# First four merge levels of a triangular inverse on 32x32 blocks at four places of TensorE's array, and three small edits around it

## What is computed

```python
def gated_deltanet(h, w_in, conv_w, a_log, dt_bias, norm_w, w_out):
    proj = h @ w_in                                   # q, k, v, z and two small gates
    ...
    q = l2norm(q) * (GDN_HEAD_DIM ** -0.5)
    k = l2norm(k)
    ...
    o = chunk_gated_delta_rule(q, k, v, g, beta)
    o = o * lax.rsqrt(jnp.mean(o * o, axis=-1, keepdims=True) + RMS_EPS) * norm_w
    o = o * jax.nn.silu(z)
    return o @ w_out

def chunk_gated_delta_rule(q, k, v, g, beta):
    ...
    m = jnp.where(strict, jnp.einsum("bhnid,bhnjd->bhnij", k_beta, k) * decay, 0.0)
    a_mat = jnp.eye(CHUNK, dtype=q.dtype) + m
    u = lax.linalg.triangular_solve(a_mat, v_beta, left_side=True, lower=True)
    w = lax.linalg.triangular_solve(a_mat, k_beta * jnp.exp(g)[..., None], left_side=True, lower=True)
```

## Time and profile before

| | |
|---|---|
| time, 3 runs | 1297.12 us median (1296.31 to 1297.67) |
| profiled execution, its own time | 1297.02 us |
| its span in the profile | 1295.2 us |
| TensorE (PE) busy | 1258.4 us, 97% |
| VectorE (DVE) busy | 994.9 us, 77% |
| ScalarE (ACT) busy | 685.0 us, 53% |
| granted TensorE clock, mean | 0.996 of full speed |

### The profile page before, as it was taken

The page is one execution under the profiler, slowest core; times in us unless marked ns, Lnnn a source line. Parts: engine busy times, 40 slices in busy tenths (PEclk is TensorE's granted clock), DMA queues, the critical chain, the costliest instruction groups (busy, mean ns, idle before and its releaser), DMA issues.

```text
span 1295.2 us, 29136 instructions
## 1 busy us (share of the span) xinstructions
PE 1258.4 (97%) x10579; PEld 1210.5 (93%) x10579; DVE 994.9 (77%) x1817; ACT 685.0 (53%) x1116; POOL 53.7 (4%) x93
## 2 busy tenths in 40 slices
PE   9999998999999999999999999999999999999997
PEld 8989898999999899999998899998899999999986
DVE  6897748998878898998877787775566668777654
ACT  6865435655543544665553555554365565645541
POOL 0002000000001000000000000000000000000000
PEclk9999999999999999999999999999999999999999
DMA  7550123588888588388875366665455335666651
GB/s 269 160 150 2 52 82 115 199 301 278 294 281 278 200 291 270 113 305 278 276 252 167 98 198 184 186 197 192 135 179 180 125 106 178 189 184 179 227 177 34
DMA packets 64778, 244.74 MB, mean 189 GB/s; under 512 B 7200, under 2 KB 8512, under 8 KB 64704
## 3 DMA queue, kind: packets, MB, share of 16 engines
q1 hardware_dynamic: 54048, 204.77, 48.7%
q0 software_dynamic: 10656, 38.93, 9.5%
HBM read 242.63 MB, written 1.05 MB: 188 GB/s over the span
## 4 chain that ended last, share of the span: by engine, by line
PE 73%; DVE 6%; DMA 2%; issue 1%; ACT 1%; DVEq 0%; POOLq 0%; ACTq 0%
PE ps L1778 17%; PE ps L1779 17%; PE ps L1780 16%; PE ps L2137 9%; PE ps L2138 5%; DMA ring<-in_ada_w 2%; DVE wlo L410 1%; PE ps L1793 1%; PE ps L1799 1%; PE ps L1794 1%; DVE ring L1298 1%; PE ps L2282 1%; PE ps L2284 1%; PE ps L2283 1%; DVE xb L1423 1%
## 5 line engine op out<-in xcount | busy, mean ns | idle before, releaser
L1778 PE MATMUL ps<-hhi,whi 128*128 128x258 f32 (+4 forms) x1952 | 557.6, 286 | 5.0 <-DVE hlo L1038 1.9
L1779 PE MATMUL ps<-hlo,whi 128*128 128x258 f32 (+4 forms) x1952 | 553.8, 284 | 0.0
L1780 PE MATMUL ps<-hhi,wlo 128*128 128x258 f32 (+4 forms) x1952 | 553.3, 283 | 0.0
L403 ACT ACTIVATE whi<-raw 128x1024 fp32r<-128x1024 f32 (+1 forms) x360 | 399.9, 1113 | 285.2 <-PE ps L1780 166.3
L410 DVE TENSOR_TENSOR wlo<-raw,whi 128x1024 fp32r<-128x1024 f32 (+1 forms) x360 | 463.4, 1292 | 84.8 <-ACT whi L403 82.7
L1778 PEld LDWEIGHTS ps<-hhi,whi 128*128 128x128 f32 x1952 | 369.4, 189 | 7.5 <-issue 4.6
L1780 PEld LDWEIGHTS ps<-hhi,wlo 128*128 128x128 f32 x1952 | 370.5, 190 | 0.0
L1779 PEld LDWEIGHTS ps<-hlo,whi 128*128 128x128 f32 x1952 | 370.2, 190 | 0.3
L2137 PE MATMUL ps<-aboth,whi 128*128 128x512 f32 x528 | 185.6, 396 | 0.0
L2138 PE MATMUL ps<-aboth,wlo 128*128 128x256 f32 x528 | 147.9, 280 | 0.0
L2137 PEld LDWEIGHTS ps<-aboth,whi 128*128 128x128 f32 x528 | 99.3, 188 | 23.2
(11 more groups left out here) (416 smaller groups left out, 1557.4 us busy)
## 6 DMA issues: line engine op xcount, KB each, us to landing
raw<-in_w_up SPq DMA_DIRECT2D x176, 512.0 KB, 3.9
raw<-in_w_down SPq DMA_DIRECT2D x64, 704.0 KB, 4.7
ring<-in_ada_w POOLq DMA_DIRECT2D x72, 512.0 KB, 5.3
raw<-in_w_mix SPq DMA_DIRECT2D x48, 512.0 KB, 3.6
raw<-in_w_a_in SPq DMA_DIRECT2D x32, 512.0 KB, 3.6
raw<-in_w_b_cx SPq DMA_DIRECT2D x16, 512.0 KB, 5.2
raw<-in_w_a_out SPq DMA_DIRECT2D x8, 512.0 KB, 3.6
raw<-in_w_b_gate SPq DMA_DIRECT2D x8, 512.0 KB, 4.7
```

The source lines that it names most:

```text
L403: nc.scalar.activation(whi[:, s, 0:blocks * P], raw[:, s, 0:blocks * P], ACT.Copy).then_inc(hi_split, 1)
L1778: nc.tensor.matmul(out, whi[:, s, w], rhi(k0 + k), start=first and k == 0, stop=False)
L1779: nc.tensor.matmul(out, whi[:, s, w], rlo(k0 + k), start=False, stop=False)
L1780: ins = nc.tensor.matmul(out, wlo[:, s, w], rhi(k0 + k), start=False, stop=last and k == blocks - 1)
```

## The change

1. **Levels 0 to 4 on 32x32 blocks.** A new constant FINE = 4 and four QUARTERS of the partitions. Up to level 4 the pieces are at most 32x32, so the four diagonal quarters of a block sit at four partition ranges with 32 columns each. x_mm and y_mm of levels 1 to 4 and the turns of levels 0 to 3 become 16 matmuls of 32x32x32 at four places of the array instead of 8 of 64x64x64 at two. mask_x, add_y and the copy of the turn handle 128 columns instead of 256. Behind level 4 the result has to go back to the 64-column layout of level 5: add_y of level 4 writes to `ex` and a second VectorE operation spreads it over 64 columns with a 0/1 mask (the constant C_SPREAD). `first_inverse` takes four operations on 32 partitions and 128 columns instead of two on 64 partitions and 256 columns.
2. **Norms' turn one unit on.** The transpose of `norms` moves behind `one(U_V + 3)`, and VectorE's factors behind `d_v(U_V + 3)`.
3. **Shared odd squares.** Of the odd blocks ScalarE squares the last four, and VectorE the first four (semaphore sq_dve). The transpose inside the last gate unit moves from k = 3 to k = 2.
4. **Gate units with 262 columns.** The eight units of z take 262 columns (`z_unit`) instead of 272.

```diff
@@ -34,6 +34,9 @@
 TOP, HALF = LEVELS - 1, P // 2
 LOW, HIGH = slice(0, HALF), slice(HALF, P)
 HALVES = (LOW, HIGH)
+FINE, QUARTER = 4, P // 4
+QUARTERS = [slice(q * QUARTER, (q + 1) * QUARTER) for q in range(4)]
+SMALL = QUARTERS[0]
 
 
 STEPS = [
...
@@ -604,6 +611,9 @@
                 if l == 0:
                     act.wait_ge(qg_ready, OPENS_AT[g] + 1)
                 act.wait_ge(mm_turn, i + 1)
+                if l < FINE:
+                    nc.scalar.activation(gt[:, b0:b0 + n, SMALL], quarters_at(turn_bank(i), n), ACT.Copy).then_inc(tu_ready, 1)
+                    return
                 part = LOW if l == TOP - 1 else slice(0, P)
                 nc.scalar.activation(gt[part, b0:b0 + n, LOW], halves_at(turn_bank(i), n, part), ACT.Copy).then_inc(tu_ready, 1)
 
...
@@ -695,7 +705,7 @@
 
                 s = u % SLOTS
                 act.wait_ge(unit_done, u + 1)
-                nc.scalar.activation(zs[:, u - U_Z, :], ps[s][:, TOK - N_A:TOK], ACT.Silu).then_inc(tiles_read, 1)
+                nc.scalar.activation(zs[:, u - U_Z, :], ps[s][:, 0:N_A], ACT.Silu).then_inc(tiles_read, 1)
                 split_hi(act, u // SLOTS + 1, s, KT)
 
 
@@ -716,7 +726,7 @@
 
 
             act.wait_ge(o_read, 5)
-            nc.scalar.activation(ex[:, 1:MB:2, :], ot[:, 1:MB:2, :], ACT.Square).then_inc(sq_gdn, 1)
+            nc.scalar.activation(ex[:, HEADS + 1:MB:2, :], ot[:, HEADS + 1:MB:2, :], ACT.Square).then_inc(sq_gdn, 1)
             a_z(U_Z + 7)
             for h in range(HEADS):
                 act.wait_ge(og_ready, h + 1)
@@ -1148,6 +1158,7 @@
             dve.wait_ge(mm_rows, 1)
             nc.vector.tensor_copy(norms[:, :], ps[7][:, 0:P]).then_inc(rows_read, 1)
             d_v(U_V + 2)
+            d_v(U_V + 3)
 
 
             dve.wait_ge(mm_norm, 1)
@@ -1159,7 +1170,7 @@
             mine(nc.vector.tensor_scalar(S_(13), rq, float(P) ** -0.5, None, ALU.mult))
             step(nc.vector.tensor_tensor(S_(15), rk, S_(10), ALU.mult))
             nc.vector.scalar_tensor_tensor(S_(16), S_(12), -1.0, S_(9), ALU.mult, ALU.mult).then_inc(cols_ready, 1)
-            for u in range(U_V + 3, U_Z - 1):
+            for u in range(U_V + 4, U_Z - 1):
                 d_v(u)
 
             def gate_diff(g):
@@ -1190,10 +1201,10 @@
 
                 b0, n = GROUPS[g]
                 dve.wait_ge(m_ready, OPENS_AT[g] + 1)
-                for half in HALVES:
-                    last = nc.vector.tensor_tensor(gu[half, b0:b0 + n, LOW], bn[half, b0:b0 + n, half], bcast(cm[half, C_PAIR, LOW], n), ALU.mult)
+                for q in QUARTERS:
+                    last = nc.vector.tensor_tensor(gu[q, b0:b0 + n, SMALL], bn[q, b0:b0 + n, q], bcast(cm[q, C_PAIR, SMALL], n), ALU.mult)
                 step(last)
-                nc.vector.tensor_tensor(gu[:, b0:b0 + n, LOW], gu[:, b0:b0 + n, LOW], bcast(cm[:, C_DIAG, LOW], n), ALU.add).then_inc(gu0_ready, 1)
+                nc.vector.tensor_tensor(gu[:, b0:b0 + n, SMALL], gu[:, b0:b0 + n, SMALL], bcast(cm[:, C_DIAG, SMALL], n), ALU.add).then_inc(gu0_ready, 1)
 
             def mask_x(m):
                 (l, g), j = m, MERGE_AT[m]
@@ -1203,6 +1214,9 @@
                     dve.wait_ge(ca_ready, OPENS_AT[g] + 1)
                 if l == TOP:
                     nc.vector.tensor_scalar(ex[HIGH, b0:b0 + n, LOW], halves_at(ps[j % 2], n, HIGH), -1.0, None, ALU.mult).then_inc(x_ready, 1)
+                elif l <= FINE:
+                    nc.vector.tensor_tensor(ex[:, b0:b0 + n, SMALL], quarters_at(ps[j % 2], n),
+                                            bcast(cm[:, C_LEVEL + l, SMALL], n), ALU.mult).then_inc(x_ready, 1)
                 else:
                     nc.vector.tensor_tensor(ex[:, b0:b0 + n, LOW], halves_at(ps[j % 2], n),
                                             bcast(cm[:, C_LEVEL + l, LOW], n), ALU.mult).then_inc(x_ready, 1)
@@ -1213,6 +1227,14 @@
                 dve.wait_ge(mm_y, j + 1)
                 if l == TOP:
                     nc.vector.tensor_copy(gu[LOW, b0:b0 + n, HIGH], halves_at(y_bank(j), n, LOW)).then_inc(gu_ready, 1)
+                elif l < FINE:
+                    nc.vector.tensor_tensor(gu[:, b0:b0 + n, SMALL], gu[:, b0:b0 + n, SMALL], quarters_at(y_bank(j), n), ALU.add).then_inc(gu_ready, 1)
+                elif l == FINE:
+                    step(nc.vector.tensor_tensor(ex[:, b0:b0 + n, SMALL], gu[:, b0:b0 + n, SMALL], quarters_at(y_bank(j), n), ALU.add))
+                    nc.vector.tensor_tensor(gu[:, b0:b0 + n, LOW].rearrange("p b (c t) -> p b c t", t=QUARTER),
+                                            ex[:, b0:b0 + n, SMALL].unsqueeze(2).to_broadcast([P, n, 2, QUARTER]),
+                                            bcast(cm[:, C_SPREAD, HIGH], n).rearrange("p b (c t) -> p b c t", t=QUARTER),
+                                            ALU.mult).then_inc(gu_ready, 1)
                 else:
                     nc.vector.tensor_tensor(gu[:, b0:b0 + n, LOW], gu[:, b0:b0 + n, LOW],
                                             halves_at(y_bank(j), n), ALU.add).then_inc(gu_ready, 1)
@@ -1261,6 +1283,8 @@
             d_z(U_Z + 6)
 
 
+            dve.wait_ge(o_read, 4)
+            nc.vector.tensor_tensor(ex[:, 1:HEADS:2, :], ot[:, 1:HEADS:2, :], ot[:, 1:HEADS:2, :], ALU.mult).then_inc(sq_dve, 1)
             dve.wait_ge(mm_rows, 2)
             nc.vector.tensor_copy(norms[:, :], ps[5][:, 0:P]).then_inc(rows_read, 1)
             dve.wait_ge(mm_norm, 2)
@@ -1823,6 +1847,10 @@
 
                 a_unit(u // SLOTS, u % SLOTS)
 
+            def z_unit(u, k_wait=None):
+
+                unit(u // SLOTS, u % SLOTS, KT, N_A, lambda k: hhi[:, k, TOK - N_A:TOK], lambda k: hlo[:, k, TOK - N_A:TOK], k_wait=k_wait)
+
             def a_unit(t, s):
                 unit(t, s, KT, TOK, lambda k: hhi[:, k, 0:TOK], lambda k: hlo[:, k, 0:TOK])
 
@@ -1890,9 +1918,10 @@
             pe.wait_ge(sq_gdn, U_V + 1)
             qk_sums(MB, 2 * NBLK).then_inc(mm_rows, 1)
             one(U_V + 2)
+            one(U_V + 3)
             pe.wait_ge(rows_read, 1)
             nc.tensor.transpose(ps[7][:, P:2 * P], norms[:, :], ident).then_inc(mm_norm, 1)
-            for u in range(U_V + 3, U_Z - 1):
+            for u in range(U_V + 4, U_Z - 1):
                 one(u)
 
             def spread(bank, b0, n, which):
@@ -1951,9 +1980,13 @@
                     to = slice((b - b0) * HALF, (b - b0 + 1) * HALF)
                     if l == TOP:
                         last = nc.tensor.matmul(ps[j % 2][HIGH, to], bn[LOW, b, HIGH], gt[LOW, b, LOW], start=True, stop=True)
-                    else:
+                    elif l > FINE:
                         for half in HALVES:
                             last = nc.tensor.matmul(ps[j % 2][half, to], bn[half, b, half], gt[half, b, LOW], start=True, stop=True)
+                    else:
+                        to = QUARTERS[b - b0]
+                        for q in QUARTERS:
+                            last = nc.tensor.matmul(ps[j % 2][q, to], bn[q, b, q], gt[q, b, SMALL], start=True, stop=True)
                 last.then_inc(mm_x, 1)
 
             def y_mm(m):
...
@@ -1994,6 +2031,11 @@
                     if l == TOP - 1:
                         last = nc.tensor.transpose(turn_bank(i)[LOW, to], gu[LOW, b, LOW], ident[LOW, LOW])
                         continue
+                    if l < FINE:
+                        to = QUARTERS[b - b0]
+                        for q in QUARTERS:
+                            last = nc.tensor.matmul(turn_bank(i)[q, to], gu[q, b, SMALL], ident[q, q], start=True, stop=True)
+                        continue
                     for half in HALVES:
                         last = nc.tensor.matmul(turn_bank(i)[half, to], gu[half, b, LOW], ident[half, half], start=True, stop=True)
                 last.then_inc(mm_turn, 1)
...
@@ -2101,11 +2145,11 @@
 
             def o_norms(k):
 
-                if k == 3:
+                if k == 2:
                     pe.wait_ge(rows_read, 2)
                     nc.tensor.transpose(ps[5][:, P:2 * P], norms[:, :], ident).then_inc(mm_norm, 1)
 
-            unit((U_Z + 7) // SLOTS, (U_Z + 7) % SLOTS, KT, TOK, lambda k: hhi[:, k, 0:TOK], lambda k: hlo[:, k, 0:TOK], k_wait=o_norms)
+            z_unit(U_Z + 7, o_norms)
             pe.wait_ge(tiles_read, SLOTS + U_Z + KT)
             pe.wait_ge(cols_ready, 2)
             for g in (4, 0, 1, 2, 3):
@@ -2441,11 +2485,16 @@
     i, j = np.arange(P)[:, None], np.arange(P)[None, :]
     same = i // META == j // META
     out = [i == j, np.full((P, P), 1.0 / D), np.ones((P, P)), i <= j, same & (i <= j), same]
-    i, j = i % HALF, np.where(j < HALF, j, P)
+    p, full = i, j
+    i, j = p % QUARTER, np.where(full < QUARTER, full, P)
     out.append(-1.0 * ((i >> 1 == j >> 1) & (i < j)))
     for l in range(1, TOP):
+        if l > FINE:
+            i, j = p % HALF, np.where(full < HALF, full, P)
```

(8 more changed lines are left out.)

20 lines of the change are left out of this document (14 added, 6 removed).

## The result

The changed kernel takes 1313.0 us (median, 1310.4 to 1314.6) against 1296.7 us (1296.2 to 1297.7): ratio 1.0121, 95% interval 1.0109 to 1.0134. It is 16 us slower, and 24 us above the forecast.

The account below looks back on a forecast made before the run. TensorE, busy for 97% of the span, was taken as the bound. Gains of 6.35 (inverse), 0 (norms), 1.0 (output norm) and 0.4 us (gate units) sum to 7.75: from 1297.02 to 1289.3, median 1289.4, range 1287.0 to 1295.5.

Parts of the forecast that it names:

- the price of a product: In the inverse, 32 records of a 32x32 product at four places take 0.253 us in place of 0.467.
- the sum of part 1: Inverse on 32x32 blocks: 10.8 us out of TensorE's queue, of which 6.35 us arrive, added stretch by stretch.
- stretch 2: Second stretch of the inverse: 2.73 us less, TensorE's 5.4 us still bound against VectorE's 3.8; gain 2.7 us.
- 8 records at 21 ns: Where level 6's x_mm and level 5's y_mm overlap, 8 records start in 0.17 us: 25 ns is no floor there.
- a record has a floor: Rival for the inverse: records follow no faster than 25 ns, a product takes 0.80 us; about 1310 us, chance 0.14.
- The clock: Rival in the inverse's waits: 3 us at 1.2 GHz would cost 1.5 us; chance of two or more 0.03.
- Mask and add on 128 columns: VectorE's operations in the inverse: 0.29 us each on 128 columns, saving 0.135 us each against 256 columns.
- The four operations of level 0: Inverse's entry: four 128-column VectorE operations replace two of 256, costing 0.3 us more; TensorE's wait grows to about 1.5.
- The waits of the turns for VectorE's adds: Sign in the inverse: new TensorE waits of 3 to 5 us together, mostly behind level 3.
- Part 2: Norms' transpose one unit later: TensorE's 1.4 us wait goes but moves to a later one; gain 0, at most 1.4.
- the wait for L1187's successor: TensorE's wait at group 0's gate products (L1901), growing from 0.7 to about 2.1 us.
- Parts 3 and 4: Output norm's shared squares with the earlier transpose gain 1.0 us, narrower gate units between inverse and norm 0.4 us.

Follow-up runs that it names:

- inv_only: The kernel before with only the 32x32 blocks of levels 0 to 4; norms, squares and gate units as before: 1312.2 us, ratio 1.0112.
- bench_mix: The kernel before plus longer written-out measuring pieces, small products alone or mixed with full ones, then 64x64 ones; run once: 1664 small records took 47.6 us.
- wide96: The changed kernel with every 32x32 matmul moving 96 columns instead of 32, instruction count kept, inverse not computed: 1314.9 us, ratio 1.0134.
- norms_only: The kernel before with only the norms' transpose and VectorE's weight split one unit later: 1298.0 us, ratio 1.0007.
- bench: The kernel before plus independent products behind the first layer norm, written out and looped; run once: 512 small records took 12.7 us written out, 7.9 us looped.
- pairs: The changed kernel with each four-block 32x32 product made of 8 matmuls with 64 moving columns, not 16 with 32; inverse not computed: 1295.7 us, ratio 0.999.

## Why the prediction was wrong

**The step that failed** is the one from the price of a product to the sum of part 1: "The rows don't decide this fully", and then 0.253 us times 48. Its mechanism was right (four places work at once, 16 records do not wait for a floor), and the size of a product in a burst nearly so: 0.28 to 0.31 us in place of 0.253. The sum took this price as one that holds over 48 products. It does not, because a 32x32 product has twice the instructions of a 64x64 one, and TensorE's instructions come at 27 to 32 ns a record on average (3.45 to 4.1 us for 128). The sum had no term for their supply. For stretch 2 it asked for 223 + 12 x 16 = 415 records in 5.4 us, 13 ns a record. In the kernel after 128 records come in 3.8 to 4.1 us (restarts from 120.27 to 143.72 us), so these needed 12 to 13 us. Part 1 was forecast to gain 6.35 us and cost 14.5 (`inv_only`). No long run of the trace before was faster than 29 ns a record (rows 4; the token sums' 26 ns from rows 5 go over only 32 records). That is the 64x64 products' own speed, the same in a loop without any fetching, and that the supply lies so near to it is chance; but it meant that the trace before could not show the limit. I weighed it against 8 records at 21 ns, and a burst out of what lies ready can't refute an average.

The Trainium skill, Runtime: NRT & Kernel Launch, Instruction fetch mechanics, says that instructions come in blocks of 16 KiB, 256 at a time, that the next block is fetched while the current one runs, and that crossing a boundary is "mostly hidden". The stops 128 records apart agree with the block; "mostly hidden" holds in `bench_mix` at 29.3 ns a record, over 573 records also at 27.5 ns, and fails at 9.9 and 15 ns, with stops of 1.5 to 3.6 us.

**The rival "a record has a floor"** gave 1310 us and came nearest, by luck: for another reason. A single record has no floor at 25 ns (128 in 1.27 us), so the rule that the prediction weighed, some 25 ns for each matmul (the Trainium skill, TensorE: Matmul & The Clock Gate, Back-to-back issue gap), isn't borne out by these runs; the average has a floor, of nearly the same size. I gave this rival 0.14; by the rows it deserved more, since no run of 16 records or longer in the trace before was faster than 26 ns a record.

**The clock.** It did fall, by the mean clock of the windows for about 34 us, far more than the prediction's 3 us, in the stretch of the stops, which were not foreseen. Yet it costs next to nothing: `wide96` keeps it at 1.00 there and takes as long, since at 1.2 GHz a product (0.42 to 0.45 us apart at 125.20 to 126.50 us) is still faster than its instructions arrive (0.9 us).

**VectorE.** Mask and add on 128 columns were priced at 290 ns; in the kernel after and in `wide96` the masks take 290 and the adds 287 ns. The group of the masks in `wide96`:

```profile
L1218 DVE TENSOR_TENSOR ex<-ps,cm 128x128 f32<-128x128 f32 x15 | 4.4, 290 | 14.3 <-PE ps L1990 14.3
```

The four operations of level 0 were priced at 4 x 0.29 us; they take 464 ns each on average in the kernel after, and 2.6 us the four in the last wide group. TensorE's wait for them is 1.3 us, where 1.5 was forecast. The waits of the turns for VectorE's adds (3 to 5 us forecast) hardly came (0.6 and 0.8 us), because TensorE itself was late: VectorE waited for it, in `wide96` 14.3 us before the masks of the row above.

**Part 2** gains nothing, as forecast, and may cost up to 2 us (`norms_only`). The place of the new wait was wrong: the wait for L1187's successor stays at 0.7 us, and the sums of group 1, one step earlier, wait for 1.7 us, where the prediction had 2.1 us for L1187's successor. **Parts 3 and 4** were forecast at 1.4 us and gave 1.2 (0 to 2.3); the last sums' wait is 0.7 us where 0.6 was named.

## What to carry to other kernels

Before replacing matmuls by more and smaller ones, count instructions, not only columns: in these runs written-out code on TensorE gets 128 records (weight load and matmul) in some 3.7 us, 29 ns a record, and a plan that asks for less time per record over more than the 217 records that lay ready is paid at that rate. Such work can lie beside wide matmuls (27.5 ns a record in the mean ran without a stop), or in a loop, which ran without fetching, at 15.5 ns a record. The 64x64 products at two places, at 29.3 ns, lie just at the limit: in long runs little is gained by making them shorter unless the number of instructions falls too.

## What the runs showed of the hardware

- The supply does not follow the clock: 128 small records take 1.27 us at full and 1.93 us at half clock, and in `bench_mix` restarts lie 3.45 to 4.0 us apart. The first gap of each measuring piece is longer, 4.55 us in `bench` and 4.83 us in `bench_mix`, with 118 and 112 GB/s of DMA traffic beside it. The starved stretch is 66.1 us long at a clock of 1.00 and 65.7 us at 0.74.
- It does not follow the work strictly either way: in `pairs`, where the 128 records take longer, restarts lie up to 4.6 us apart (122.36, 126.78, 131.39 us).
- Two packets at most seem to lie ready: 217 small records ran at the start of both measuring pieces, before the first stop.
- In the kernel after the clock stood at 0.50 for 3.5 us from 94 us on, behind the waits of 1.7 and 0.7 us, and so it did in `wide96`, while `norms_only` and `pairs` have the same waits there and no fall. Why is open. The third gate unit ends 0.5 us later than in `pairs` (113.14 against 112.60 us), so this fall explains little of the loss.
- The transfer is the smaller part of the 3.66 us between packets. The 13 packets of `bench_mix` hold 1.9% of 16 engines' 47.64 us, 1.1 us each. In slices of 0.2 us they start at 251.4 to 251.6 and 254.8 to 255.0 us, some 1.1 us behind the restarts at 250.42 and 253.87 us, and TensorE restarts 1.2 to 1.4 us behind a packet's end. Only one packet is under way at a time there. What passes ahead of a packet and behind it was not tried.
